# Five block products of seven in each six pairs of the up projections, and one scaling moved behind the down projection

## The chip, the cores and the metric

The kernel runs on one core of one Trainium2 chip, as one program. The metric is the device time of an execution in microseconds (us). Five engines matter: TensorE (PE in the rows, its weight loads PEld), VectorE (DVE), ScalarE (ACT), GpSimd (POOL) and SyncE (SP), which issues the weight transfers.

## The reference

A first block (token mixing and a convolutional feed-forward network) is followed by a second block of two layers, each with a gated feed-forward network. The change touches these two, which the kernel calls `ffn2` and `ffn3`. Everything is float32, with 512 tokens, a model width of 1024 and an inner width of 2816 = 22 x 128:

```python
def rms_norm_2(x, g):
    y = x * lax.rsqrt(jnp.mean(x * x, axis=-1, keepdims=True) + RMS_EPS)
    return y * g

def swiglu_ffn(h, w13, w2):
    g, u = jnp.split(h @ w13, 2, axis=-1)
    return (jax.nn.silu(g) * u) @ w2
# h = h + swiglu_ffn(rms_norm_2(h, ffn_norm_g), w13, w2)
```

## The kernel before, in words

Activations lie transposed: channels on the 128 partitions, 512 tokens along the free dimension (`xT`, eight tiles). Every weight product is made in three passes of a high and a low float32r part (`passes`, lines 382 to 384). So each unit of weights (128 output columns of all 1024 rows, 512 KB) is loaded into one of four buffers `raw`, its high part copied by ACT (`split_hi`, L369) into one of two `whi`, its low part made by DVE (`split_lo`, L377) into one of two `wlo`.

The inverse root of the norm, `rs`, is one number for each token, so it is multiplied in behind the product: DVE evicts a gate or up tile from PSUM as `zS = ps * rs` (L894). ACT applies Silu to the gate half (`act_silu_gate`, L796), DVE multiplies by the up half into `h` (`dve_product`, L899).

An up projection has 22 pairs of a gate and an up unit. Two pairs stand ahead of a loop, two behind it; the loop has `ROUNDS` = 3 iterations of six pairs, ordered by `PATTERN`. False is an ordinary pair: 2 units x 8 slices x 3 passes = 48 matmuls of 512 columns (`pe_pair`). True is a pair by block products (`pe_seven`): the pair is cut in 2 x 2 blocks (halves of the 1024 rows by gate and up columns; the input by halves of the rows and of the tokens), and seven products m1 to m7 of sums of blocks replace eight. A product is 4 slices x 3 passes = 12 matmuls of 256 columns, a pair 84. TensorE takes them in the order m1, m6, m2, m5, m3, m7, m4.

The sums of weight blocks of the next seven pair are prepared one pair ahead, between the additions of the present one. On DVE that is: three sums (`dve_w_sums`, L868 to L871), the low part of two of them (L875, behind ACT's high part L800), the low part of the gate unit (L881), one more difference (L884) and its low part (L888, behind ACT's L804). m1 of the next pair waits for `sums_lo`, which L881 completes. L800 waits for m5 of the present pair, since m5 still reads `w_hi`. So one set of sums can be made ahead and no more.

The seven products are put together by DVE: L912, L913, L916 (behind m2 and m5), L928 (m3), L935 and L937 (m7), L939 (m4), each 256 columns wide. L930 scales the gate half by `rs`, L941 the up half.

In the down projections (`dve_residual`) one of eight output tiles is finished every 22 slices, and DVE adds it to `xT` (L556), which ACT and DVE split again for the next stage (L452, L458).

Of the kernel before, what the change touches and what calls it, by code (L numbers as in the profile page):

```python
# [17 lines left out]
ALU = mybir.AluOpType  # L18
# [6 lines left out]
KT = D // P  # L25
# [94 lines left out]
FIRST = {}  # L120
# [112 lines left out]
    XPART0[_s] = KT * len(XPART0)  # L233
HU, HT = UNIT // 2, T // 2
LAST_PAIRS = 2 * FT - 4
PATTERN = (False, True, True, False, True, True)
ROUNDS = (FT - 4) // len(PATTERN)
SEVENS = ROUNDS * sum(PATTERN)
SEVEN0 = {"ffn2_up": 0, "ffn3_up": 1}
# [6 lines left out]
def build(nc, A, cst_d, out_d, known):  # L246
    ctx = ExitStack()
    with ctx:
# [3 lines left out]
        def sem(name):  # L252
            return ctx.enter_context(nc.semaphore(name))
# [45 lines left out]
        x_read = sem("x_read")  # L299
        sums_made, sums_hi, sums_lo = sem("sums_made"), sem("sums_hi"), sem("sums_lo")  # L300
        block_done, block_kept, block_added = sem("block_done"), sem("block_kept"), sem("block_added")
        S.sems["acc_free"] = acc_free
        x_loaded = [sem(f"x_loaded{i}") for i in range(TT)]
        cst0_loaded, cst_loaded = sem("cst0_loaded"), sem("cst_loaded")
# [239 lines left out]
        def dve_residual(dve, stage, thirds, gain, following=None):  # L544
            per, np_, tiles = round_of(thirds)
            n0 = TILE0[stage]

            def body(i, begun):
                for j in range(per):
                    if begun and j == per - 1:  # L550
                        dve_regain(dve, begun, range(5))
                    if j % np_ == np_ - 1:
                        m = j // np_
                        dve.wait_ge(unit_used, FIRST[stage] + j + 1 + per * i)
                        x = tile_of(xT, m + tiles * i)
                        v.tensor_tensor(x, acc(m), x, ALU.add).then_inc(acc_free, 1)  # L556
                    if begun and j == per - 1:
                        dve_regain(dve, begun, range(5, KT))
                        if not thirds:
                            dve_last_square(dve, stage)  # L560
                    split_lo(dve, FIRST[stage] + j + 2, i, per)
                    if j % np_ == np_ - 1 and gain:
                        dve.wait_ge(acc_free, n0 + m + 3 + tiles * i)
                        dve_gained(dve, gain, m + tiles * i, XPART0[gain] + m + 1 + tiles * i)
            rounds(dve, stage, KT // tiles, body, following)
# [142 lines left out]
                    also()  # L708

        def pe_seven(pe, stage, u, i, s, in_row):  # L710
            n0, a0 = TILE0[stage] + u - 2, nth(stage, i, s, 7) - 7
            u += FIRST[stage]

            def multiply(n, w, x):
                (xh, xl), wh, wl = x_part(x), w_part(whi, w_hi, u, w), w_part(wlo, w_lo, u, w)
                for k in range(4):
                    cols = slice(k * P, (k + 1) * P)
                    last = passes(seven_bank(stage, n), wh[:, cols], wl[:, cols], xh[:, k, :], xl[:, k, :],
                                  k == 0, k == 3)
                return last  # L720
            if in_row:
                pe.wait_ge(block_added, a0 + 2)
            else:
                pe.wait_ge(acc_free, in_units(n0 + 2, i))
            pe.wait_ge(sums_lo, nth(stage, i, s, 2) + 2)
            multiply("m1", "g0", "x11").then_inc(block_done, 1)
            for n in X_SUMS:
                pe.wait_ge(*after(f"{stage} {n} lo"))
            multiply("m6", "s2", "t2")
            multiply("m2", "g1", "x21").then_inc(unit_used, 1)  # L730
            if in_row:
                pe.wait_ge(block_added, a0 + 6)
            multiply("m5", "s1", "t1").then_inc(block_done, 1)
            pe.wait_ge(lo_split, in_units(u + 1, i))
            multiply("m3", "s4", "x22").then_inc(block_done, 1)
            pe.wait_ge(lo_split, in_units(u + 2, i))
            multiply("m7", "s3", "t3").then_inc(block_done, 1)
            if in_row:
                pe.wait_ge(block_added, a0 + 7)
            multiply("m4", "u1", "t4").then_inc(unit_used, 1)  # L740

        def pe_up_seven(pe, stage, name, gain, residual):
# [51 lines left out]
        def act_silu_gate(act, stage, u, i, zS, yg):  # L794
            act.wait_ge(acc_free, in_units(TILE0[stage] + u + 3, i))
            a.activation(yg[:, u // 2 % 2, :], zS[:, 0, :], ACT.Silu).then_inc(gated, 1)  # L796

        def act_two_sums_hi(act, stage, i, s):
            act.wait_ge(sums_made, nth(stage, i, s, 4) + 2)
            a.activation(w_hi[:, 0:2, :], xg[:, :, :], ACT.Copy).then_inc(sums_hi, 1)  # L800
# [5 lines left out]
        def act_pair(act, stage, n, i, zS, yg):  # L806
            special, following = PATTERN[n], PATTERN[(n + 1) % len(PATTERN)]
            u, s, per = 4 + 2 * n, sum(PATTERN[:n]), 2 * len(PATTERN)
            b0 = nth(stage, i, s, 4)
            if special:  # L810
                act.wait_ge(sums_made, b0 + 3)
            split_hi(act, FIRST[stage] + u + 1, i, per)
            if special:
                act.wait_ge(block_done, b0 + 1)
                act.wait_ge(acc_free, in_units(TILE0[stage] + u + 1, i))
                a.activation(kept["m1"], seven_bank(stage, "m1"), ACT.Copy).then_inc(block_kept, 1)
                if following:
                    act.wait_ge(block_done, b0 + 2)
            if following:
                act_two_sums_hi(act, stage, i, s + special)  # L820
            split_hi(act, FIRST[stage] + u + 2, i, per)
            if special and following:
                act.wait_ge(block_done, b0 + 3)
                act_last_sum_hi(act, stage, u + 2, i, s + special)
            act_silu_gate(act, stage, u, i, zS, yg)
            if following and not special:
                act_last_sum_hi(act, stage, u + 2, i, s + special)

        def act_begin_seven(act, stage, name, gain):
            a.preload_act_table_set("natural_log_exp_and_others")  # L830
# [4 lines left out]
        def act_up_seven(act, stage, h, h_hi, zS, yg):  # L835
            u0 = FIRST[stage]
            a.preload_act_table_set("silu_and_others")
            act_silu_gate(act, stage, 0, None, zS, yg)
            act_x_sums_hi(act, stage, ("t1",))
            split_hi(act, u0 + 3)  # L840
            act_x_sums_hi(act, stage, ("t3", "t2"))
            split_hi(act, u0 + 4)
            act_silu_gate(act, stage, 2, None, zS, yg)
            act_x_sums_hi(act, stage, ("t4",))
            with act.Fori(0, ROUNDS) as i:
                for n in range(len(PATTERN)):
                    act_pair(act, stage, n, i, zS, yg)
            u = LAST_PAIRS
            split_hi(act, u0 + u + 1)
            for j, tiles in enumerate((range(0, 6), range(6, 12), range(12, 17), range(17, 21))):  # L850
                for m in tiles:
                    act_product_hi(act, stage, m, h, h_hi)
                split_hi(act, u0 + u + j + 2)
                if j % 2 == 0:
                    act_silu_gate(act, stage, u + j, None, zS, yg)
            act_product_hi(act, stage, FT - 1, h, h_hi)
# [32 lines left out]
                            ALU.subtract).then_inc(lo_split, 1)  # L889

        def dve_up_unit(dve, stage, u, i, j, odd, zS):
            dve.wait_ge(unit_used, in_units(FIRST[stage] + u + j + 1, i))
            dve.wait_ge(prod_done, in_pairs(PAIR0[stage] + u // 2 + 2, i))
            v.tensor_tensor(zS[:, j, :], pair_bank(stage, odd, j), rs[:, :], ALU.mult).then_inc(acc_free, 1)  # L894

        def dve_product(dve, stage, u, i, h, zS, yg):
            dve.wait_ge(acc_free, in_units(TILE0[stage] + u + 4, i))
# [4 lines left out]
        def dve_pair(dve, stage, n, i, h, zS, yg):  # L902
            special, following = PATTERN[n], PATTERN[(n + 1) % len(PATTERN)]
            u, s, per = 4 + 2 * n, sum(PATTERN[:n]), 2 * len(PATTERN)
            u0, b0, a0 = FIRST[stage] + u, nth(stage, i, s, 4), nth(stage, i, s, 7)
            split_lo(dve, u0 + 1, i, per)
            if following:
                dve_w_sums(dve, stage, u + 2, i, s + special)
# [24 lines left out]
            if special:  # L933
                dve.wait_ge(block_done, b0 + 4)
                v.tensor_tensor(kept["u3"], seven_bank(stage, "m7"), kept["u2"], ALU.add).then_inc(block_added, 1)  # L935
                dve.wait_ge(block_added, a0 + 5)
                v.tensor_tensor(zS[:, 1, HT:T], seven_bank(stage, "m5"), kept["u3"], ALU.add).then_inc(block_added, 1)  # L937
                dve.wait_ge(unit_used, in_units(u0 + 2, i))
                v.tensor_tensor(zS[:, 1, 0:HT], seven_bank(stage, "m4"), kept["u3"], ALU.add).then_inc(block_added, 1)  # L939
                dve.wait_ge(block_added, a0 + 7)  # L940
                v.tensor_tensor(zS[:, 1, :], zS[:, 1, :], rs[:, :], ALU.mult).then_inc(acc_free, 1)  # L941
            else:
                dve_up_unit(dve, stage, u, i, 1, 0, zS)
            dve_product(dve, stage, u, i, h, zS, yg)
# [2090 lines left out]
```

## Time and profile before

| | |
|---|---|
| time, three runs | 1831.75 us median (1831.74 to 1834.98) |
| profiled execution | 1835.28 us, its span 1833.5 us |
| TensorE's granted clock | 0.999 |
| busy PE, DVE, ACT | 98%, 62%, 42% |
| DMA | 161.19 MB, 88 GB/s |
| up projection `ffn2`, loop | 945.3 to 1131.6 us, three rounds of 62.1 us |

A row of the timeline gives start and duration from the span's start. The time between two starts can be shorter than the duration, since instructions of one engine overlap at their ends. Ends of matmuls are modelled, so for TensorE the distance between starts is to be read.

### The profile page before, as it was taken

How to read it: one execution, taken by the hardware profiler on the slowest of the kernel's cores; microseconds unless marked ns; L12 is line 12 of the kernel's file. 1: busy time of each engine (PE TensorE's matmuls, PEld its weight loads, DVE VectorE, ACT ScalarE, POOL GpSimd, SP SyncE). 2: the span in 40 equal slices, each digit the busy share in tenths (PEclk: the TensorE clock that was granted, in tenths of full speed). 3: DMA queues.
4: the chain of work that ended last, by engine and by line, in shares of the span. 5: the costliest groups of instructions: out<-in, count | busy, mean ns of one | idle time of the engine just before them, and what ended most of it. 6: DMA issues, size and time to landing. Idle time of an engine off the chain costs nothing.

```text
span 1833.5 us, 29524 instructions
## 1 busy us (share of the span) xinstructions
PE 1801.9 (98%) x10927; PEld 1499.9 (82%) x10927; DVE 1128.0 (62%) x1670; ACT 775.4 (42%) x1155; POOL 146.9 (8%) x134
## 2 busy tenths in 40 slices
PE   7999999999999999999999999999999999999998
PEld 6787676688888888888889999888776789999887
DVE  6553677467676633445588888533757398888422
ACT  6635436454444422322354335323555363345322
POOL 0030001111111100000200000001000200000010
PEclk9999999999999999999999999999999999999999
DMA  6311212133333333333333333333230233333331
GB/s 196 81 38 48 59 36 81 35 92 95 100 92 102 87 97 102 94 103 93 98 98 102 96 102 100 95 95 105 77 91 1 69 92 104 103 102 96 94 101 66
DMA packets 309240, 161.19 MB, mean 88 GB/s; under 512 B 12688, under 2 KB 306832, under 8 KB 309024
## 3 DMA queue, kind: packets, MB, share of 16 engines
q1 hardware_dynamic: 308080, 157.28, 30.0%
q0 software_dynamic: 640, 2.17, 0.4%
q8 instruction: 61, 1.00, 0.2%
q10 hardware_dynamic: 432, 0.52, 0.1%
q14 instruction: 27, 0.22, 0.0%
HBM read 157.85 MB, written 2.10 MB: 87 GB/s over the span
## 4 chain that ended last, share of the span: by engine, by line
PE 96%; DVE 2%; ACT 1%; issue 1%; DMA 0%; ACTq 0%; DVEq 0%
PE ps L382 28%; PE ps L384 28%; PE ps L383 28%; PE ps L2125 1%; PE ps L1536 1%; PE ps L2442 1%; PE ps L2443 1%; PE ps L2116 1%; PE ps L1447 1%; PE ps L1853 1%; PE ps L1269 1%; PE ps L1797 1%; PE ps L1841 0%; PE ps L2222 0%; PE ps L2223 0%
## 5 line engine op out<-in xcount | busy, mean ns | idle before, releaser
L382 PE MATMUL ps<-xhi,whi 128*128 128x512 f32 (+1 forms) x1464 | 558.7, 382 | 2.0 <-DVE xlo L1176 1.1
L384 PE MATMUL ps<-xhi,wlo 128*128 128x512 f32 (+1 forms) x1464 | 550.2, 376 | 0.0
L383 PE MATMUL ps<-xlo,whi 128*128 128x512 f32 (+1 forms) x1464 | 550.0, 376 | 0.0
L369 ACT ACTIVATE whi<-raw 128x1024 fp32r<-128x1024 f32 (+2 forms) x297 | 308.4, 1039 | 528.2 <-PE ps L384 527.8
L377 DVE TENSOR_TENSOR wlo<-raw,whi 128x1024 fp32r<-128x1024 f32 (+2 forms) x273 | 335.3, 1228 | 231.2 <-ACT whi L369 231.2
L382 PEld LDWEIGHTS ps<-xhi,whi 128*128 128x128 f32 x1464 | 275.8, 188 | 55.9 <-issue 4.6
L383 PEld LDWEIGHTS ps<-xlo,whi 128*128 128x128 f32 x1464 | 275.9, 188 | 50.9 <-issue 3.1
L384 PEld LDWEIGHTS ps<-xhi,wlo 128*128 128x128 f32 x1464 | 275.7, 188 | 50.3
L576 POOL TENSOR_TENSOR ssq<-ssq,sq 128x512 f32<-128x512 f32 x45 | 72.1, 1602 | 990.5 <-ACT sq L523 990.5
L384 PE MATMUL ps<-h_lo,wlo 128*128 128x512 f32 x352 | 136.9, 389 | 0.0
L382 PE MATMUL ps<-h_lo,whi 128*128 128x512 f32 x352 | 136.9, 389 | 0.0
L383 PE MATMUL ps<-h_hi,whi 128*128 128x512 f32 x352 | 136.9, 389 | 0.0
L556 DVE TENSOR_TENSOR xT<-ps,xT 128x512 f32<-128x512 f32 (+1 forms) x48 | 33.2, 691 | 120.1 <-PE ps L384 120.1
L382 PEld LDWEIGHTS ps<-h_lo,whi 128*128 128x128 f32 x352 | 66.1, 188 | 13.9
L384 PEld LDWEIGHTS ps<-h_lo,wlo 128*128 128x128 f32 x352 | 66.1, 188 | 13.7
L383 PEld LDWEIGHTS ps<-h_hi,whi 128*128 128x128 f32 x352 | 66.1, 188 | 13.6
L382 PE MATMUL ps<-h_hi,whi 128*128 128x512 f32 x176 | 68.5, 389 | 0.0
L383 PE MATMUL ps<-h_lo,whi 128*128 128x512 f32 x176 | 68.5, 389 | 0.0
L384 PE MATMUL ps<-h_hi,wlo 128*128 128x512 f32 x176 | 68.5, 389 | 0.0
L800 ACT ACTIVATE w_hi<-xg 128x1024 fp32r<-128x1024 f32 x24 | 25.5, 1063 | 89.3 <-PE ps L384 48.3
L648 DVE TENSOR_TENSOR zS<-ps,rs 128x512 f32<-128x512 f32 x44 | 30.4, 692 | 43.8 <-PE ps L384 41.4
L458 DVE SCALAR_TENSOR_TENSOR xlo<-xT,pcol,xhi 128x512 fp32r<-128x512 f32 (+1 forms) x48 | 47.0, 1009 | 12.6 <-ACT xhi L452 12.6
(389 smaller groups left out, 2760.6 us busy)
## 6 DMA issues: line engine op xcount, KB each, us to landing
raw<-in_conv_ffn_w SPq DMA_DIRECT2D x52, 512.0 KB, 3.8
raw<-in_mla_ffn_w SPq DMA_DIRECT2D x52, 512.0 KB, 3.8
raw<-in_w_up SPq DMA_DIRECT2D x44, 512.0 KB, 3.8
raw<-in_w_in SPq DMA_DIRECT2D x28, 512.0 KB, 3.8
raw<-in_conv_w_in SPq DMA_DIRECT2D x24, 512.0 KB, 3.8
raw<-in_w_down SPq DMA_DIRECT2D x16, 448.0 KB, 3.7
raw<-in_conv_ffn_w SPq DMA_DIRECT2D x16, 448.0 KB, 3.7
raw<-in_mla_ffn_w SPq DMA_DIRECT2D x16, 448.0 KB, 3.7
```

Of the source, the lines that this page charges most:

```text
L369: a.activation(whi[:, u % PARTS, 0:n], raw[:, u % RAW, 0:n], ACT.Copy).then_inc(hi_split, 1)
L377: e.tensor_tensor(wlo[:, u % PARTS, 0:n], raw[:, u % RAW, 0:n], f32(whi[:, u % PARTS, 0:n]), ALU.subtract).then_inc(lo_split, 1)
L382: t_.matmul(out, wh, xh, start=first, stop=False)
L383: t_.matmul(out, wh, xl, start=False, stop=False)
L384: return t_.matmul(out, wl, xh, start=False, stop=last)
L458: v.scalar_tensor_tensor(tile_of(xlo, k), tile_of(xT, k), gain_of(name, k), f32(tile_of(xhi, k)), ALU.mult, ALU.subtract).then_inc(x_lo, 1)
L556: v.tensor_tensor(x, acc(m), x, ALU.add).then_inc(acc_free, 1)
L576: g.tensor_tensor(ssq[:, :], ssq[:, :], sq[:, m, :], ALU.add).then_inc(summed, 1)
L648: v.tensor_tensor(z, acc(j), rs[:, :], ALU.mult).then_inc(acc_free, 1)
L800: a.activation(w_hi[:, 0:2, :], xg[:, :, :], ACT.Copy).then_inc(sums_hi, 1)
L1269: t_.matmul(out, C("hsum"), sq[:, i % 2, :], start=True, stop=True).then_inc(*step("pe", f"{name} sum{i} full"))
L1447: last = t_.matmul(chunk(out, n)[rows], chunk(lhs, c)[rows], chunk(rhs, c)[rows], start=True, stop=True)
```

## The change

`PATTERN` has five pairs of seven products in six. The up half is no longer scaled in either kind of pair: in an ordinary pair ACT copies it out of PSUM (`act_up_half`), in a pair of seven L941 goes. Since `rs` belongs to the token, it can be multiplied in behind the down projection: `dve_residual` scales each output tile (L561 of the new kernel) and then adds it to `xT` (L563). PSUM banks of m4 are now guarded by `acc_free`.

```diff
-PATTERN = (False, True, True, False, True, True)
+PATTERN = (False, True, True, True, True, True)
...
+            scaled = {"ffn2_down": 0, "ffn3_down": KT}.get(stage)
...
-                        v.tensor_tensor(x, acc(m), x, ALU.add).then_inc(acc_free, 1)
+                        if scaled is None:
+                            v.tensor_tensor(x, acc(m), x, ALU.add).then_inc(acc_free, 1)
+                        else:
+                            v.tensor_tensor(xg[:, m % 2, :], acc(m), rs[:, :], ALU.mult).then_inc(out_scaled, 1)
+                            dve.wait_ge(out_scaled, scaled + m + 1 + tiles * i)
+                            v.tensor_tensor(x, xg[:, m % 2, :], x, ALU.add).then_inc(acc_free, 1)
...
             if in_row:
-                pe.wait_ge(block_added, a0 + 7)
+                pe.wait_ge(acc_free, in_units(n0 + 4, i))
             multiply("m4", "u1", "t4").then_inc(unit_used, 1)
...
+        def act_up_half(act, stage, u, i, odd, zS):
+            act.wait_ge(unit_used, in_units(FIRST[stage] + u + 2, i))
+            act.wait_ge(prod_done, in_pairs(PAIR0[stage] + u // 2 + 2, i))
+            a.activation(zS[:, 1, :], pair_bank(stage, odd, 1), ACT.Copy).then_inc(acc_free, 1)
...
             if following and not special:
                 act_last_sum_hi(act, stage, u + 2, i, s + special)
+            if not special:
+                act_up_half(act, stage, u, i, 0, zS)
...
                 for m in tiles:
                     act_product_hi(act, stage, m, h, h_hi)
+                if j % 2:
+                    act_up_half(act, stage, u + j - 1, None, j // 2, zS)
...
         def dve_up_unit(dve, stage, u, i, j, odd, zS):
-            dve.wait_ge(unit_used, in_units(FIRST[stage] + u + j + 1, i))
-            dve.wait_ge(prod_done, in_pairs(PAIR0[stage] + u // 2 + 2, i))
-            v.tensor_tensor(zS[:, j, :], pair_bank(stage, odd, j), rs[:, :], ALU.mult).then_inc(acc_free, 1)
+            if j == 0:
+                dve.wait_ge(unit_used, in_units(FIRST[stage] + u + 1, i))
+                dve.wait_ge(prod_done, in_pairs(PAIR0[stage] + u // 2 + 2, i))
+                v.tensor_tensor(zS[:, 0, :], pair_bank(stage, odd, 0), rs[:, :], ALU.mult).then_inc(acc_free, 1)
...
-                v.tensor_tensor(zS[:, 1, 0:HT], seven_bank(stage, "m4"), kept["u3"], ALU.add).then_inc(block_added, 1)
-                dve.wait_ge(block_added, a0 + 7)
-                v.tensor_tensor(zS[:, 1, :], zS[:, 1, :], rs[:, :], ALU.mult).then_inc(acc_free, 1)
+                v.tensor_tensor(zS[:, 1, 0:HT], seven_bank(stage, "m4"), kept["u3"], ALU.add).then_inc(acc_free, 1)
+                dve.wait_ge(block_added, a0 + 6)
```

DVE at the end of a pair of seven, as the program of before has it (`ISA` and `REGISTER_ALU` are steps of the sequencer alone):

```order
L939 TENSOR_TENSOR zS<-ps,sq 128x256 [waits unit_used]
L940 REGISTER_ALU
L941 TENSOR_TENSOR zS<-zS,rs 128x512 [waits block_added]
L897 REGISTER_ALU
L898 REGISTER_ALU [waits acc_free]
L899 ISA [waits gated]
L899 TENSOR_TENSOR h<-yg,zS 128x512
```

And the same place in the changed kernel, whose line numbers are 19 higher here:

```order
L958 TENSOR_TENSOR zS<-ps,sq 128x256 [waits unit_used]
L959 REGISTER_ALU
L916 REGISTER_ALU [waits block_added]
L917 REGISTER_ALU [waits acc_free]
L918 ISA [waits gated]
L918 TENSOR_TENSOR h<-yg,zS 128x512
```

The scaling is gone and the product stands directly behind the last addition, with its waits.

ACT at the end of an ordinary pair in the loop, from the Silu to the high part of the next pair's up unit, before:

```order
L796 ACTIVATE yg<-zS 128x512 [waits acc_free]
L803 REGISTER_ALU
L804 ACTIVATE w_hi<-raw 128x512 [waits sums_made]
L811 REGISTER_ALU
L366 REGISTER_ALU [waits sums_made]
L368 REGISTER_ALU [waits unit_loaded0]
L369 ACTIVATE whi<-raw 128x1024 [waits unit_used]
```

And in the changed kernel:

```order
L803 ACTIVATE yg<-zS 128x512 [waits acc_free]
L815 REGISTER_ALU
L816 ACTIVATE w_hi<-raw 128x512 [waits sums_made]
L806 REGISTER_ALU
L807 ISA [waits unit_used]
L808 ACTIVATE zS<-ps 128x512 [waits prod_done]
L823 REGISTER_ALU
L367 REGISTER_ALU [waits sums_made]
L370 ACTIVATE whi<-raw 128x1024 [waits unit_used,unit_loaded0]
```

The copy out of PSUM (L808) stands between them and waits for the pair's last matmul; the high part of the next up unit is queued behind it.

## Rows read from the trace of the kernel before

**Rows 1.** The page: the chain that ended last, by engine
```profile
PE 96%; DVE 2%; ACT 1%; issue 1%; DMA 0%; ACTq 0%; DVEq 0%
```

**Rows 2.** Windows: stretch, its us, busy (x instructions) by engine, clock, DMA
```profile
956.18:966.25 10.07, 10.07 (x85) 10.07 (x84) 8.40 (x12) 3.46 (x4) 0.00 (x0) 1.00 0.36 104
976.33:987.24 10.91, 10.91 (x50) 9.02 (x49) 9.13 (x12) 4.35 (x5) 0.00 (x0) 1.00 0.29 85
945.30:1007.40 62.10, 62.10 (x434) 58.34 (x433) 53.38 (x81) 24.10 (x30) 0.00 (x0) 1.00 0.34 98
```

**Rows 3.** Timeline, DVE: start us, us, line, operation, shape, idle before
```profile
957.33 0.69 DVE L899 TENSOR_TENSOR h<-yg,zS 128x512 f32 x1 [0.26 <-DVE zS L894]
957.94 1.22 DVE L377 TENSOR_TENSOR wlo<-raw,whi 128x1024 fp32r<-128x1024 f32 x1
959.07 0.69 DVE L868 TENSOR_TENSOR xg<-raw 128x512 f32<-128x512 f32 x1
959.79 0.69 DVE L870 TENSOR_TENSOR xg<-xg,raw 128x512 f32<-128x512 f32 x1
960.40 0.69 DVE L871 TENSOR_TENSOR raw<-raw 128x512 f32<-128x512 f32 x1
961.00 0.42 DVE L912 TENSOR_TENSOR sq<-ps,sq 128x256 f32<-128x256 f32 x1
961.34 0.42 DVE L913 TENSOR_TENSOR zS<-ps,sq 128x256 f32<-128x256 f32 x1
962.24 0.42 DVE L916 TENSOR_TENSOR sq<-ps,sq 128x256 f32<-128x256 f32 x1 [0.48 <-PE ps L384]
963.32 1.23 DVE L875 TENSOR_TENSOR w_lo<-xg,w_hi 128x1024 fp32r<-128x1024 f32 x1 [0.66 <-ACT w_hi L800]
964.47 1.22 DVE L881 TENSOR_TENSOR wlo<-raw,whi 128x1024 fp32r<-128x1024 f32 x1
965.72 0.69 DVE L884 TENSOR_TENSOR raw<-raw,xg 128x512 f32<-128x512 f32 x1
966.33 0.42 DVE L928 TENSOR_TENSOR zS<-ps,sq 128x256 f32<-128x256 f32 x1
966.78 0.69 DVE L930 TENSOR_TENSOR zS<-zS,rs 128x512 f32<-128x512 f32 x1
967.39 0.68 DVE L888 TENSOR_TENSOR w_lo<-raw,w_hi 128x512 fp32r<-128x512 f32 x1
967.99 0.42 DVE L935 TENSOR_TENSOR sq<-ps,sq 128x256 f32<-128x256 f32 x1
968.44 0.42 DVE L937 TENSOR_TENSOR zS<-ps,sq 128x256 f32<-128x256 f32 x1
968.78 0.41 DVE L939 TENSOR_TENSOR zS<-ps,sq 128x256 f32<-128x256 f32 x1
969.23 0.69 DVE L941 TENSOR_TENSOR zS<-zS,rs 128x512 f32<-128x512 f32 x1
970.18 0.69 DVE L899 TENSOR_TENSOR h<-yg,zS 128x512 f32 x1 [0.25 <-DVE zS L941]
970.79 1.22 DVE L377 TENSOR_TENSOR wlo<-raw,whi 128x1024 fp32r<-128x1024 f32 x1
```

**Rows 4.** Timeline, ACT, same stretch
```profile
956.38 1.06 ACT L369 ACTIVATE whi<-raw 128x1024 fp32r<-128x1024 f32 x1 [1.52 <-PE ps L384]
962.23 1.06 ACT L800 ACTIVATE w_hi<-xg 128x1024 fp32r<-128x1024 f32 x1 [4.03 <-PE ps L384]
966.45 0.64 ACT L804 ACTIVATE w_hi<-raw 128x512 fp32r<-128x512 f32 x1 [2.20 <-DVE raw L884]
```

**Rows 5.** The page, costliest groups: one weight load
```profile
L382 PEld LDWEIGHTS ps<-xhi,whi 128*128 128x128 f32 x1464 | 275.8, 188 | 55.9 <-issue 4.6
```

**Rows 6.** Timeline, end of the second network's first down projection
```profile
1273.42 0.69 DVE L556 TENSOR_TENSOR xT<-ps,xT 128x512 f32 x1 [2.56 <-PE ps L384]
...
1275.99 1.32 DVE L458 SCALAR_TENSOR_TENSOR xlo<-xT,pcol,xhi  x1 [0.38 <-ACT xhi L452]
...
1277.86 0.39 PE L382 MATMUL ps<-xhi,whi 128*128 128x512 f32 x1
```

**Rows 7.** Chain of waits in order of time, the kernel's end
```profile
1821.54 0.70 DVE xT L556
```

More of the change, by code:

```diff
@@ L301, in build @@
         block_done, block_kept, block_added = sem("block_done"), sem("block_kept"), sem("block_added")
+        out_scaled = sem("out_scaled")
         S.sems["acc_free"] = acc_free
@@ L710, in pe_seven @@
         def pe_seven(pe, stage, u, i, s, in_row):
-            n0, a0 = TILE0[stage] + u - 2, nth(stage, i, s, 7) - 7
+            n0, a0 = TILE0[stage] + u - 2, nth(stage, i, s, 6) - 6
             u += FIRST[stage]
@@ L839, in act_up_seven @@
             act_x_sums_hi(act, stage, ("t1",))
+            act_up_half(act, stage, 0, None, 0, zS)
             split_hi(act, u0 + 3)
@@ L844, in act_up_seven @@
             act_x_sums_hi(act, stage, ("t4",))
+            act_up_half(act, stage, 2, None, 1, zS)
             with act.Fori(0, ROUNDS) as i:
@@ L904, in dve_pair @@
             u, s, per = 4 + 2 * n, sum(PATTERN[:n]), 2 * len(PATTERN)
-            u0, b0, a0 = FIRST[stage] + u, nth(stage, i, s, 4), nth(stage, i, s, 7)
+            u0, b0, a0 = FIRST[stage] + u, nth(stage, i, s, 4), nth(stage, i, s, 6)
             split_lo(dve, u0 + 1, i, per)
```

## The prediction

> **What bounds the kernel now.** I read the chain of waits first: TensorE holds 96% of it, DVE 2% [rows 1]. A change pays only where TensorE gets less to do or is made to wait. Next I read the windows over the loop of the `ffn2` up projection. A pair by seven products takes TensorE 10.07 us, an ordinary pair 10.91 us, and a round of four and two 62.10 us, with no gap: 4 x 10.07 + 2 x 10.91 = 62.1 [rows 2]. In that round DVE is busy 53.4 us and ACT 24.1 us [rows 2]. By these averages nothing but TensorE matters. The timeline of DVE through one pair of seven that also prepares the next says something else [rows 3]. From its first instruction (L377 at 957.94) to that of the next pair (970.79) it takes 12.85 us, longer than TensorE's 10.07. That goes well today because such a pair is never followed by another: the next pair of seven prepares nothing, and the ordinary pair leaves DVE time. The change puts four such pairs in a row. So the forecast rests on one number, how long DVE needs for such a pair when it is the one that is late.
>
> **TensorE's gain.** One ordinary pair in each round becomes one of seven: 10.91 - 10.07 = 0.84 us [rows 2]. There are three rounds in each of two networks, so 6 x 0.84 = 5.0 us, if nothing waits.
>
> **DVE's period in a row of preparing pairs.** Count start to start [rows 3]. In the 12.85 us stand two waits that are TensorE's and ACT's doing and not DVE's: L916 starts 0.90 behind L913, waiting for m5, and L875 starts 1.08 behind L916, waiting for ACT's L800, which itself waited for m5 [rows 4]. Without a wait a 256-column addition is followed after 0.34 (L912 to L913). That takes off 0.56 + 0.74 = 1.30 and leaves 11.55. The change takes L941 away. From L939 to the product it is now 1.40 (968.78 to 970.18): 0.45 to L941, its 0.69, and a gap of 0.25-0.26 before the product, which waits for the result in front of it. Without L941 the product waits for L939 instead: 0.42 + 0.25 = 0.67. Saved 0.73, so the period is 11.55 - 0.73 = 10.82 us. That is still 0.75 more than TensorE's 10.07.
>
> Would the two waits stay, or others take their place? Take L875 of one pair as zero. L881 ends at 1.15 + 1.22 = 2.37 and releases m1 of the next pair; its m5, the fourth product, is done 6.05 later (962.23 - 956.18, from the start of the pair to ACT's L800 [rows 2, 4]), at 8.4. DVE's L870 of that pair comes at 7.47 (963.32 to 970.79) - 0.73 + 1.85 = 8.59 and ends at 9.28; ACT's 1.06 brings 10.4, and L875 is due at 10.82. So L800 is hidden, by 0.4 us. L804 comes 1.40 behind L884's start (0.69, 0.03, 0.64 and 0.03 [rows 3, 4]) and L888 is due at 1.67: hidden by 0.27. m7 and m4 of that pair are over by 12.9, and its L939 is due at 10.82 + 5.46 = 16.3. No other wait is late next.
>
> **Where TensorE waits.** Let a round's first pair of seven start at zero. Its L875 starts at 963.32 - 956.18 = 7.14 [rows 2, 3] and is still set by TensorE's m5. The second pair's follows at 17.96, the third's at 28.78, the fourth's at 39.60. The fourth's L881 ends 2.37 later, at 41.97; for the way to TensorE I add 0.1, between 0.03 (ACT's L800 ends at 963.29, L875 starts at 963.32 [rows 3, 4]) and 0.22, that plus a weight load of 0.19 no longer hidden [rows 5]. The fifth pair starts at 42.07 instead of 4 x 10.07 = 40.3. TensorE loses 1.75 to 1.8 us: about 0.25 before the third pair and 0.75 before the fourth and the fifth each. Before the second it loses nothing (L881 ends at 9.5, TensorE is free at 10.07). The fifth prepares nothing, and the ordinary pair gives DVE time to be early again. A round becomes 62.10 - 0.84 + 1.75 = 63.0 us, +0.91; six rounds +5.5 us.
>
> The Trainium skill, page "VectorE: DVE Perf Modes", section "The DRAIN you can't avoid", says that semaphores between chained Vector instructions cost nothing extra. By it, L941 is worth only the spacing of two such instructions. This trace disagrees: L930 comes 0.45 behind L928, for whose result it waits, where an addition without such a wait comes after 0.34, and the product comes 0.95 behind L941 [rows 3]. By the rule the sum would be that of the upper bound below, +8.6 us.
>
> **Bounds of the saving.** The trace does not show the product directly behind a 256-column addition. At least L941's plain spacing goes, 0.61 (L884 to L928): period 10.94, loss 2.11, a round +1.27, together +8.6 with the ends below. At most the product comes 0.45 behind L939 as L941 did, saved 0.95: period 10.60, loss 1.09, +2.5 us in all. I take 0.73, since the product stands 0.25 or 0.26 behind the end of what it waits for in both of its rows, behind an eviction and behind L941 [rows 3]. With the way to TensorE at 0.03 or 0.22 the ends are +2.1 and +9.3.
>
> **The up half on ACT.** In an ordinary pair ACT copies 512 columns, some 0.65 us like L804 [rows 4], instead of DVE's 0.69; the product waits for either and starts at about the same time, 957.3. Queued behind the copy is L369, which started at 956.38 [rows 4] and now starts near 957.0, ending at 958.0; L377 follows at 958.1 instead of 957.94. L916 waits 0.48 for m5 anyway [rows 3], which hides the 0.15. Without that cover it would be 0.15 x 6 = 0.9 us. In the pairs ahead of and behind the loop the copy delays a `split_hi` by 0.65, with several microseconds until TensorE wants it. I set all of this at zero. The copy's further wait, for the last product, was over a pair earlier. The new guard of m4 waits for L939 of the pair before, which is when the old one opened.
>
> **The down projections.** Sixteen tiles get one more DVE instruction of 0.69, with the addition behind it waiting for it; behind that stand the low parts of the weights. A tile is 22 x 3 = 66 matmuls of 10.91 / 48 = 0.227 us [rows 2], so one comes every 15 us, and fourteen of them are free. At the kernel's end the addition is on the chain [rows 7]: +0.69 + 0.03 = 0.7 us. At the end of `ffn2` the last tile's low part starts at 1275.99 and ends at 1277.31, and TensorE wants it at 1277.86 [rows 6]. The addition comes 0.94 later in a loop (0.69 and the gap of 0.25), so the part ends near 1278.1: +0.3 us. It could be 0 or 0.9. Ends together +1.0.
>
> **The sum.** +5.5 + 1.0 = +6.5 us: the profiled execution of 1835.28 us would become 1841.8. It stands 3.5 above the median of the runs, and the steps are the same in both, so I lay the sum on the median: 1831.75 + 6.5 = 1838.2 us.
>
> **Rivals.** The averages decide (0.12). DVE's work in a round goes from 53.4 to about 51.7 us: the seven pair's 11.5 against the ordinary one's 9.1 [rows 2, 3], less six scalings of 0.69. That is far under TensorE's 61.3. If the preparation can be early enough, the gain of 5.0 stays less the ends of 1.0: 1827.7 us, faster. For it: DVE idles 8.7 us a round today [rows 2]. Against it: those idle times lie in other pairs, and L800 cannot start before m5. Its point is a period of 10.24 us; below that no pair waits.
>
> A smaller period that just eats the gain (0.12): at 10.46 us the loss is 0.67 a round and the total is nothing, 1832 us. It would take 0.36 less than I count, if starts close up when DVE never idles. Nothing in the rows closes up so far: every 512-column instruction without a wait takes 0.60 to 0.61 [rows 3].
>
> The handshakes with ACT and TensorE stay (0.04). If the 1.30 us of waits stand in each pair even when DVE is late, the period is 12.12, the loss 5.65 a round, +28.9 + 1.0: 1861.6 us. The margins of 0.4 and 0.27 speak against it.
>
> **How the numbers follow.** My forecast has 0.72. Its own range is 1833.9 to 1841.1 us. The range given is 1831 to 1842: it takes in the case of no change and leaves out the averages (0.12) and the handshakes (0.04). A measurement tells 0.2%, 3.7 us, from no change. Faster holds the averages and a little, 0.13. Same, to 1835.4, holds the smaller period and the low end of my own range, 0.16. Slower is 0.71.
>
> **What would show it.** In the profile after, the windows of a round show 63.0 us (61.3 if the averages are right). TensorE's first matmul of the third, fourth and fifth pair of seven has idle time before it, ended by DVE's `wlo` of the gate unit, of some 0.25, 0.75 and 0.75 us. The `w_lo` instruction of two halves starts 10.8 us apart from pair to pair and waits for ACT only in the first. The product starts 0.67 behind the last addition. The last `xT` comes 0.7 later behind the last matmul. I am wrong if the period is under 10.5, or if TensorE waits at m3, m7 or m5 rather than at m1.

## The result, and the profile after

The changed kernel takes 1843.22 us (median of five runs, 1840.95 to 1845.16), the kernel before 1833.38 us beside it (five runs, 1831.74 to 1834.98). The ratio is 1.0051, with a 95% interval of 1.0035 to 1.0068: slower by 9.4 us, between 6.4 and 12.5. Forecast were +6.5 us and 1838.2 us, with a range to 1842. So the sign and the mechanism came out, and the size was 3 us short. The median of before, from three runs 1831.75 us, moved up by 1.6 us with two more.

First the page after: the chain by engine, which answers [rows 1], and TensorE's largest group with its idle time and what ended it.

```profile
PE 85%; DVE 9%; issue 3%; ACT 2%; DVEq 0%; DMA 0%; ACTq 0%
L383 PE MATMUL ps<-xhi,whi 128*128 128x512 f32 (+1 forms) x1416 | 536.5, 379 | 8.0 <-DVE wlo L899 5.7
```

DVE's share went from 2% to 9%. The 7% more are about 129 us, far more than was lost: where TensorE waits for DVE in the end, the chain runs back through DVE's whole queue.

The window of one round of `ffn2`, from the first DVE `w_lo` of the round to the same of the next, answers the third row of [rows 2]: stretch, its us, then busy (x instructions) of PE, PEld, DVE, ACT, POOL, clock, DMA share, GB/s.

```profile
960.29:1023.28 62.99, 62.07 (x470) 59.57 (x470) 56.24 (x89) 25.93 (x35) 0.00 (x0) 1.00 0.35 101
```

A round takes 62.99 us; forecast was 63.0, and the averages would have had 61.3. DVE does more in a round than before: 89 instructions and 56.2 us busy against 81 and 53.4 [rows 2]. The new pair of seven prepares the next one, as the ordinary pair did, but now the pair in front of it prepares too. The prediction had DVE's work fall to 51.7; it counted the new pair and left out the one in front. (Busy time also holds the instructions' overlapping ends, in both kernels.)

DVE's timeline through a preparing pair that follows another answers [rows 3]: start us, us, line, operation, shape, idle time before. L893 is the old L875, L899 the old L881, L918 the product.

```profile
960.29 1.23 DVE L893 TENSOR_TENSOR w_lo<-xg,w_hi 128x1024 fp32r<-128x1024 f32 x1 [0.66 <-ACT w_hi L812]
961.44 1.22 DVE L899 TENSOR_TENSOR wlo<-raw,whi 128x1024 fp32r<-128x1024 f32 x1
...
965.75 0.41 DVE L958 TENSOR_TENSOR zS<-ps,sq 128x256 f32<-128x256 f32 x1
966.42 0.69 DVE L918 TENSOR_TENSOR h<-yg,zS 128x512 f32 x1 [0.26 <-DVE zS L958]
967.03 1.22 DVE L378 TENSOR_TENSOR wlo<-raw,whi 128x1024 fp32r<-128x1024 f32 x1
968.17 0.68 DVE L886 TENSOR_TENSOR xg<-raw 128x512 f32<-128x512 f32 x1
968.89 0.69 DVE L888 TENSOR_TENSOR xg<-xg,raw 128x512 f32<-128x512 f32 x1
969.50 0.68 DVE L889 TENSOR_TENSOR raw<-raw 128x512 f32<-128x512 f32 x1
970.10 0.42 DVE L931 TENSOR_TENSOR sq<-ps,sq 128x256 f32<-128x256 f32 x1
970.43 0.41 DVE L932 TENSOR_TENSOR zS<-ps,sq 128x256 f32<-128x256 f32 x1
970.76 0.41 DVE L935 TENSOR_TENSOR sq<-ps,sq 128x256 f32<-128x256 f32 x1
971.10 1.21 DVE L893 TENSOR_TENSOR w_lo<-xg,w_hi 128x1024 fp32r<-128x1024 f32 x1
...
981.88 1.22 DVE L893 TENSOR_TENSOR w_lo<-xg,w_hi 128x1024 fp32r<-128x1024 f32 x1
...
992.66 1.22 DVE L893 TENSOR_TENSOR w_lo<-xg,w_hi 128x1024 fp32r<-128x1024 f32 x1
```

Both waits of [rows 3] are there in the first pair and gone in the next: L935 comes 0.33 behind L932, and L893 0.34 behind L935. The period is 10.81, 10.78 and 10.78 us. The product starts 0.67 behind the last addition.

What TensorE does meanwhile, by its weight loads (which are real records, while ends of matmuls are modelled), at the first matmul of the third, fourth and fifth pair of seven:

```profile
973.50 0.19 PEld L383 LDWEIGHTS ps<-xhi,whi 128*128 128x128 f32 x1 [0.24 <-DVE wlo L899]
...
984.28 0.19 PEld L383 LDWEIGHTS ps<-xhi,whi 128*128 128x128 f32 x1 [0.65 <-DVE wlo L899]
...
995.06 0.19 PEld L383 LDWEIGHTS ps<-xhi,whi 128*128 128x128 f32 x1 [0.65 <-DVE wlo L899]
```

From one of these to the next are 10.78 us, where TensorE alone needs 10.07 [rows 2]. So it loses 0.71 us and not only the 0.65 of idle time, and in the round 62.99 - 61.26 = 1.73 us (61.26 is a round without waits, 62.10 - 0.84).

The two ends that the prediction priced: the last tile of `ffn2`'s down projection, which answers [rows 6], and the chain's row at the kernel's end, which answers [rows 7], now two instructions.

```profile
1274.11 0.69 DVE L563 TENSOR_TENSOR xT<-xg,xT 128x512 f32 x1
...
1276.67 0.97 DVE L459 SCALAR_TENSOR_TENSOR xlo<-xT,pcol,xhi  x1 [0.74 <-ACT xhi L453]
...
1277.83 0.39 PE L383 MATMUL ps<-xhi,whi 128*128 128x512 f32 x1
...
1824.99 0.69 DVE L561 TENSOR_TENSOR xg<-ps,rs 128x512 f32<-128x512 f32 x1 [7.39 <-PE ps L385]
1825.72 0.69 DVE L563 TENSOR_TENSOR xT<-xg,xT 128x512 f32<-128x512 f32 x1
```

### Where the time is, section by section

Each of the five norms has its sum, one pair of matmuls (L410, now L411) that all kernels have. In the two profiled executions these sums divide the span:

| section | before | after | difference |
|---|---|---|---|
| to the first sum (code that the change leaves alone) | 393.13 | 390.11 | -3.02 |
| from there to the sum behind `ffn2` | 885.42 | 888.40 | +2.98 |
| between the two networks' sections | 197.70 | 197.74 | +0.04 |
| `ffn3`, to DVE's first instruction of the last tile | 345.29 | 348.74 | +3.45 |
| from there to the end of the span | 11.96 | 14.1 | +2.1 |

The second row is called `ffn2`'s section below. Its first 535.0 us, to the sum ahead of `ffn2` (928.10 before, 925.07 after), are other stages, the same in all ten profiles of this study to 0.04 us; its differences are those of `ffn2`.

The first row isn't the change's: the same instructions took 389.4 to 393.1 us in the ten profiles, and the profiled execution of before had a granted clock of 0.91 between 260 and 280 us, where the one of after had 1.00. Without it the spans are apart by 1839.1 - 1833.5 + 3.0 = 8.6 us. That fits the timed 9.4, and it splits into four terms:

- The loops, 2.61 + 3.04 = 5.65 us (to the last eviction of the up projections).
- The starts of the down projections, 0.42 each, 0.84 us.
- DVE's extra instruction at the end, 0.73 us (1824.99 to 1825.72).
- TensorE's last transposes, about 1.3 us in these two executions.

The second was not foreseen at all. Three engines' timelines of after at that place, ACT, DVE and the weight loads:

```profile
1153.20 0.60 ACT L808 ACTIVATE zS<-ps 128x512 f32<-128x512 f32 x1 [1.71 <-PE ps L385]
1153.69 0.95 ACT L370 ACTIVATE whi<-raw 128x896 fp32r<-128x896 f32 x1
...
1162.31 1.09 DVE L378 TENSOR_TENSOR wlo<-raw,whi 128x896 fp32r<-128x896 f32 x1
...
1163.44 0.19 PEld L383 LDWEIGHTS ps<-h_lo,whi 128*128 128x128 f32 x1 [0.51 <-DVE wlo L378]
```

And the two of before that correspond to the second and third of these rows, ACT and DVE:

```profile
1153.68 0.96 ACT L369 ACTIVATE whi<-raw 128x896 fp32r<-128x896 f32 x1 [1.77 <-PE ps L384]
...
1162.30 1.09 DVE L377 TENSOR_TENSOR wlo<-raw,whi 128x896 fp32r<-128x896 f32 x1
```

The weight load that wants it in before, with the one in front:

```profile
1163.17 0.19 PEld L384 LDWEIGHTS ps<-h_lo,wlo 128*128 128x128 f32 x1
1163.44 0.19 PEld L382 LDWEIGHTS ps<-h_lo,whi 128*128 128x128 f32 x1
```

The start times of the two kernels look alike by chance: TensorE begins this down projection at 1153.42 in before and at 1153.00 in after, so in after DVE's rows are 0.42 later against TensorE's. Before, ACT's split of a weight unit starts when TensorE has released the buffer. Now the copy of the last up half (L808) starts then, and the split 0.49 later. Behind that split stand on DVE its low part, the last product and ten low parts of `h`, and only then the low part of the down projection's third unit. In before that part was just in time: the weight load that wants it starts at 1163.44 too, 0.27 behind the load in front of it, where 0.23 is the rhythm. In after 0.69 lie between the two (1162.75 to 1163.44), so 0.42 more.

The windows of the last microseconds, after (1826 to 1839) and before (1822 to 1828):

```profile
1826.00:1832.00 6.00, 3.73 (x27) 3.41 (x26) 2.94 (x5) 4.95 (x8) 0.00 (x0) 0.77 0.13 47
1832.00:1839.00 7.00, 1.24 (x6) 0.84 (x4) 1.08 (x2) 0.69 (x1) 0.00 (x0) 0.50 0.70 262
```

```profile
1822.00:1828.00 6.00, 4.22 (x36) 3.67 (x34) 3.26 (x6) 5.59 (x9) 0.00 (x0) 1.00 0.15 57
```

In after the granted clock was 0.77 over the first of these stretches and 0.50, its lower level of 1.2 GHz, in the second; in before it stayed at 1.00 over the transposes. TensorE's rows for the last twelve, of after and of before:

```profile
1830.42 2.82 PE L2654 MATMUL ps<-cst,xT 128*128 128x128 f32 x12 [1.42 <-ACT fin L2668]
```

```profile
1826.25 1.53 PE L2636 MATMUL ps<-cst,xT 128*128 128x128 f32 x12 [1.42 <-ACT fin L2650]
```

### The profile page after: what moved, and what is told of

Same layout as the page of the kernel before. It is cut to its first block, busy times and chain, and to the rows that moved or that the text cites. A ratio compares the mean times of both kernels' runs of the same rounds, so it can differ in the third digit from the quotient of the medians.

```text
span 1839.1 us, 30175 instructions
## 1 busy us (share of the span) xinstructions
PE 1801.4 (98%) x11143; PEld 1507.3 (82%) x11143; DVE 1145.5 (62%) x1720; ACT 790.6 (43%) x1187; POOL 143.4 (8%) x134
## 4 chain that ended last, share of the span: by engine, by line
PE 85%; DVE 9%; issue 3%; ACT 2%; DVEq 0%; DMA 0%; ACTq 0%
PE ps L383 25%; PE ps L384 25%; PE ps L385 25%; PE ps L2143 1%; DVE wlo L899 1%; DVE wlo L378 1%; PE ps L1554 1%; PE ps L2460 1%; PE ps L2461 1%; PE ps L2134 1%; DVE raw L889 1%; PE ps L1465 1%; PE ps L1871 1%; DVE h_hi L966 1%; PE ps L1287 1%
## 5 line engine op out<-in xcount | busy, mean ns | idle before, releaser
L383 PE MATMUL ps<-xhi,whi 128*128 128x512 f32 (+1 forms) x1416 | 536.5, 379 | 8.0 <-DVE wlo L899 5.7
L385 PE MATMUL ps<-xhi,wlo 128*128 128x512 f32 (+1 forms) x1416 | 526.0, 371 | 0.0
L384 PE MATMUL ps<-xlo,whi 128*128 128x512 f32 (+1 forms) x1416 | 525.9, 371 | 0.0
L378 DVE TENSOR_TENSOR wlo<-raw,whi 128x1024 fp32r<-128x1024 f32 (+2 forms) x267 | 328.0, 1228 | 229.2 <-ACT whi L370 228.9
L383 PEld LDWEIGHTS ps<-xhi,whi 128*128 128x128 f32 x1416 | 266.6, 188 | 62.1 <-DVE wlo L899 9.7
L384 PEld LDWEIGHTS ps<-xlo,whi 128*128 128x128 f32 x1416 | 266.8, 188 | 46.9 <-issue 3.1
L385 PEld LDWEIGHTS ps<-xhi,wlo 128*128 128x128 f32 x1416 | 266.7, 188 | 46.5
L559 DVE TENSOR_TENSOR xT<-ps,xT 128x512 f32<-128x512 f32 (+1 forms) x32 | 22.1, 691 | 75.7 <-PE ps L385 75.7
L383 PE MATMUL ps<-t_hi,w_hi 128*128 128x256 f32 x240 | 67.9, 283 | 0.0
L384 PE MATMUL ps<-t_lo,w_hi 128*128 128x256 f32 x240 | 67.9, 283 | 0.0
```

The costliest lines, as they stand in the source:

```text
L378: e.tensor_tensor(wlo[:, u % PARTS, 0:n], raw[:, u % RAW, 0:n], f32(whi[:, u % PARTS, 0:n]), ALU.subtract).then_inc(lo_split, 1)
L383: t_.matmul(out, wh, xh, start=first, stop=False)
L384: t_.matmul(out, wh, xl, start=False, stop=False)
L385: return t_.matmul(out, wl, xh, start=False, stop=last)
```

## The experiments

The theory: in a row of preparing pairs DVE needs 10.8 us for a pair where TensorE needs 10.07, and TensorE pays the difference at m1. The rivals are that the pattern is not the cause (the scaling behind the down projections, or ACT's copy), that averages decide, and that another engine could take DVE's load at no cost. All ratios are against the kernel before, run beside on the same chip.

### Everything but the pattern

```diff
-PATTERN = (False, True, True, True, True, True)
+PATTERN = (False, True, True, False, True, True)
```

> The changed kernel with the old order of pairs (four of seven in six, never two preparing ones in a row). Theory (DVE's period in a row of preparing pairs costs the time): rounds of 62.1 us again; what stays is the rest of the change, of which the traces show 0.7 us for the second instruction at the kernel's end, 0.4 us at the start of each down projection (TensorE waits for the low part of the third unit, queued on DVE behind ten low parts of products) and perhaps 1.4 us for transposes at the granted clock 0.5 at the very end: +1.5 to +2.9 us against the kernel before. Rival (the moved scaling and ACT's copies are what costs): the time stays near that of the changed kernel, +9 us.

Measured: 1834.76 us against 1832.22, ratio 1.0010 (1.0001 to 1.0019), +1.8 us. The profile has +0.38 in `ffn2`'s section, +0.31 in `ffn3`'s and the 0.73 at the end. So the pattern carries most of the loss. The moved scaling and ACT's copy cost 1.4 us by the profile and 1.8 by the timing, whose interval runs from 0.2 to 3.5; the prediction had 1.0. The wait at the start of the down projections is there without the pattern: the page of this run has "<-DVE wlo L378 1.0" at their weight loads, as after has and before hasn't. It is the copy's or the scaling's, then. The rows above say the copy's, and in after the first scaling of an output tile (L561) starts only at 1168.55, 5 us behind that wait.

### The pattern alone

The kernel before, with the new `PATTERN`; the up half is still scaled by DVE.

> The kernel before with five pairs of seven in six and nothing else: DVE still scales the up half. Theory: the period of a preparing pair is 11.55 us when DVE is late, TensorE loses 7.14 + 3 x 11.55 + 2.47 - 40.30 = 3.96 us in a round and gains 0.84, six rounds: +18.7 us. Rival (the averages over a round decide, DVE is busy 56 of 61 us): -5.0 us.

Measured: 1855.27 us against 1832.22, ratio 1.0125 (1.0109 to 1.0140), +22.9 us. DVE's timeline, its `w_lo` instruction from pair to pair:

```profile
961.83 1.23 DVE L875 TENSOR_TENSOR w_lo<-xg,w_hi 128x1024 fp32r<-128x1024 f32 x1 [0.66 <-ACT w_hi L800]
...
973.35 1.21 DVE L875 TENSOR_TENSOR w_lo<-xg,w_hi 128x1024 fp32r<-128x1024 f32 x1
...
985.21 1.21 DVE L875 TENSOR_TENSOR w_lo<-xg,w_hi 128x1024 fp32r<-128x1024 f32 x1
...
996.72 1.21 DVE L875 TENSOR_TENSOR w_lo<-xg,w_hi 128x1024 fp32r<-128x1024 f32 x1
```

The period is 11.52, 11.86 and 11.51 us; the prediction's working gives 11.55. (In the 11.86 the product starts 0.35 later than in the others, for no reason that the trace names.) Against 10.79 with L941 gone, a 512-column instruction and its waits for results cost 0.73 us in the pair, as forecast. In the profile `ffn2`'s section is 9.71 us longer than before's and `ffn3`'s 9.05, together 18.8, which is the expectation's 18.7. The timed difference is 4 us more. In the profile 1.7 of them lie behind the last tile, 1.1 of these in the last transposes; the rest isn't found. Against the averages this run says less than its expectation has it: DVE is busy 60.1 us in a round here (the window from 961.83 to 1027.03), not 56, which is nearly TensorE's 61.3. The next run is the test of them.

### Three in a row

The kernel before, with four of six pairs as it had, in another order.

```diff
-PATTERN = (False, True, True, False, True, True)
+PATTERN = (False, True, True, True, False, True)
```

> The kernel before with its four pairs of seven of six put as three in a row and one alone, so that every count of instructions is that of before. Theory: the third pair of a row starts 7.14 + 11.55 + 2.47 - 20.15 = 1.0 us late in each round, +6.0 us in six rounds. Rival (averages): no change.

Measured: 1839.07 us against 1832.22, ratio 1.0035 (1.0022 to 1.0049), +6.4 us. This is the sharpest test of the averages: TensorE's and DVE's work in a round is what it was (DVE busy 53.8 us in both, in windows from `w_lo` to `w_lo`), and only their order differs. `ffn2`'s section is 3.02 us longer and `ffn3`'s 2.94, together 6.0 as expected. The page, TensorE's weight loads:

```profile
L382 PEld LDWEIGHTS ps<-xhi,whi 128*128 128x128 f32 x1464 | 275.5, 188 | 61.4 <-DVE wlo L881 5.7 <-issue 4.1 <-ACT mx L1399 0.8
```

TensorE loses 5.7 us to `wlo` in six rounds, one wait in each (0.96 at 975.05 in this round), where the same row of before has none [rows 5]. The averages are refuted.

### The product on GpSimd

The kernel after, with the loops' product h = silu(gate) x up taken from DVE. DVE saves about 0.9 us in each pair, and the period would come to 9.9, under TensorE's 10.07. DVE also gets a wait for the product ahead of its additions, which is not in the cut below.

```diff
+        def pool_pair_products(pool, stage, h, zS, yg):
+            with pool.Fori(0, ROUNDS) as i:
+                for n in range(len(PATTERN)):
...
+                    g.tensor_tensor(tile_of(h, in_pairs(u // 2, i)), yg[:, u // 2 % 2, :], zS[:, 1, :],
+                                    ALU.mult).then_inc(prod_done, 1)
```

> The changed kernel with the product of the gate and up half (128x512) moved from DVE to GpSimd inside the loops. Theory: DVE's period falls from 10.80 by 0.67 + 0.61 - 0.34 = 0.94 to 9.86 us, under TensorE's 10.07; rounds of 61.3 us, no wait of TensorE for the low part of the gate unit, -5.0 us and the ends of +1.5 to +2.9: 2 to 3.5 us under the kernel before. Rival (GpSimd and DVE slow each other on SBUF): DVE's instructions beside the product are longer than 0.69 and 1.22 us and the period stays above 10.07; above 10.5 nothing is gained against the kernel before.

Measured: 1843.81 us against 1832.22, ratio 1.0063 (1.0049 to 1.0077), +11.5 us, no better than after: the expectation's rival came true. The timelines of DVE and GpSimd:

```profile
965.40 1.23 DVE L378 TENSOR_TENSOR wlo<-raw,whi 128x1024 fp32r<-128x1024 f32 x1
965.74 2.03 POOL L935 TENSOR_TENSOR h<-yg,zS 128x512 f32 x1 [10.83 <-DVE zS L976]
966.54 1.78 DVE L890 TENSOR_TENSOR xg<-raw 128x512 f32<-128x512 f32 x1
```

L890 takes 1.78 us beside the product and 0.68 in the kernel after (L886 there). The product takes 2.03 where it takes 1.30 in the next experiment. The rows read as turns: GpSimd waits for L378 to end near 966.5, works until 967.77, and L890 makes its 0.6 us behind it. The period is 10.96 us. In this window DVE never idles for the added wait. The Trainium skill, page "SBUF — State Buffer", section "SBUF: two separate sides", says that GpSimd and a DVE instruction with two SBUF inputs take one pair of ports as an exclusive lock for a whole instruction. The trace agrees: the product takes 0.73 us longer and L890 1.10.

### The same, timed

The product waits until DVE has made its three weight sums, so that it falls beside the additions that read PSUM. For this DVE's own wait for the product had to go behind most of its additions, ahead of the first write into the up half of `zS`, with a wait for the Silu in its old place. The cut shows only GpSimd's new wait.

```diff
+                    if n + 2 < len(PATTERN):
+                        pool.wait_ge(sums_made, nth(stage, i, sum(PATTERN[:n + 2]), 4) + 3)
```

> The product on GpSimd as in the run before, but in the row of preparing pairs it waits for the third sum of weights of the next pair, so that it runs beside DVE's three additions out of PSUM (1.0 us) and not beside instructions with two SBUF operands. Theory (GpSimd and DVE exclude each other on SBUF pairs, the price was 1.1 us in one instruction): at most 0.45 us are left to stretch the next w_lo, the period falls from 10.95 to 9.9 to 10.3 us, TensorE waits at most 0.1 us in a round, rounds of 61.3 to 61.5 us: 2 to 3.5 us under the kernel before, 11 to 14 under the run before. Rival (DVE is stretched whatever it reads): the period stays at 10.9 and the time at that of the run before, +11 us against the kernel before.

Measured: 1834.46 us against 1833.74, ratio 1.0006 (0.9996 to 1.0015), +1.1 us: 2 to 3.5 us of gain were expected, and none came. DVE and GpSimd again:

```profile
972.16 0.42 DVE L951 TENSOR_TENSOR sq<-ps,sq 128x256 f32<-128x256 f32 x1
972.44 1.30 POOL L937 TENSOR_TENSOR h<-yg,zS 128x512 f32 x1 [9.77 <-DVE raw L893]
972.50 0.41 DVE L952 TENSOR_TENSOR zS<-ps,sq 128x256 f32<-128x256 f32 x1
972.83 0.41 DVE L955 TENSOR_TENSOR sq<-ps,sq 128x256 f32<-128x256 f32 x1
973.38 1.45 DVE L897 TENSOR_TENSOR w_lo<-xg,w_hi 128x1024 fp32r<-128x1024 f32 x1
...
983.46 1.66 DVE L897 TENSOR_TENSOR w_lo<-xg,w_hi 128x1024 fp32r<-128x1024 f32 x1
```

The additions keep their 0.41 to 0.42 us; L897, with two inputs in SBUF, is drawn out from 1.22 by what is left of the product. The periods are 10.08, 10.08 and 10.30 us, and a round, by the windows from 963.30 to 1024.81, takes 61.51 us. With DVE's period at TensorE's own, the loops gain what the prediction's averages promised, less 0.25: `ffn2`'s section is 1.4 us below before, `ffn3`'s 1.0. The periods and the round came as expected, then, and the ends take the gain back. In the profile the part from DVE's first instruction of the last tile to the span's end is 14.3 us, against 12.0 in before. DVE's extra instruction is 0.73 of that, the transposes are alike (1.53 us), and 1.6 come behind DVE's last instruction, where only the output's transfer is left: 6.6 us against 4.9. That last piece runs from 3.6 to 6.6 us in the ten profiles, and no row says why.

### The tail

The low parts of the last four `h` tiles of each up projection on GpSimd, so that DVE's low part of the third down unit is early again. Once on top of the timed product, once on the kernel after alone.

```diff
-            for m in range(16, FT):
+            for m in range(16, 18):
...
+        def pool_last_lows(pool, stage, h, h_hi, h_lo):
+            pool.wait_ge(prod_lo, PAIR0[stage] + 18 + 2)
+            for m in range(18, FT):
+                pool.wait_ge(prod_hi, PAIR0[stage] + m + 1)
+                g.tensor_tensor(h_lo[:, m, :], h[:, m, :], f32(h_hi[:, m, :]), ALU.subtract).then_inc(prod_lo, 1)
```

> The same, and the last four low parts of products (18 to 21) on GpSimd, so that DVE is free 2.4 us earlier for the low part of the down projection's third unit. Theory: TensorE's wait of 0.42 us at the start of each down projection goes, 0.8 us under the same kernel without this: 3 to 4.5 us under the kernel before. Rival (that wait is nothing, the 0.4 us come from elsewhere): no difference.

> The changed kernel with only the last four low parts moved to GpSimd. Theory: 0.8 us under the changed kernel (which is 9.4 over the kernel before by its ratio): +8.5 us, and in its trace the first output tile of each down projection 0.4 us nearer to the last gate tile. Rival: no difference, +9.4 us.

Measured with the product: 1832.90 us against 1833.74, ratio 0.9996 (0.9987 to 1.0005), where 3 to 4.5 us of gain were expected. Alone: 1841.29, ratio 1.0040 (1.0028 to 1.0053), +7.3 us where +8.5 was. The intervals, some 2 us to either side, are too wide to show 0.8 us. The profiles do: in them the two sections lose 0.37 and 0.43 us against the kernel without it, and on the kernel after 0.39 and 0.51, of 0.42 expected for each. The weight loads of the down projections in the kernel with the tail alone have no wait for DVE left, where after has "<-DVE wlo L378 1.0":

```profile
L383 PEld LDWEIGHTS ps<-h_lo,whi 128*128 128x128 f32 x352 | 66.1, 188 | 13.8
```

That settles the unforeseen term. The version with both is the best one found. By the two ratios it is 10 us faster than the change as made, and it can't be told from the kernel before.

### Without the scaling of the gate half

The kernel after without L949 in pairs of seven. This leaves a part of the computation out; it asks what becomes late next when DVE needs 0.7 us less. ACT's Silu gets a wait of its own for the addition in front, not in the cut.

```diff
-                dve.wait_ge(block_added, a0 + 4)
-                v.tensor_tensor(zS[:, 0, :], zS[:, 0, :], rs[:, :], ALU.mult).then_inc(acc_free, 1)
```

> The changed kernel with one DVE instruction less in each pair of seven: the gate half is not scaled either there (part of the computation is left out). Theory (only DVE's period counts): the period falls by 0.45 + 0.61 - 0.34 = 0.72 to 10.07 us, just TensorE's own 10.07, the three waits of a round go, rounds of 61.3 us; -5.0 us, the ends +1.5 to +2.9: 2 to 3.5 us under the kernel before, 11 to 13 under the changed one. Rival (a row of preparing pairs makes TensorE wait for ACT or for PSUM banks, whatever DVE does): rounds stay above 62.5 us and the time within 3 us of the changed kernel.

Measured: 1837.21 us against 1833.74, ratio 1.0022 (1.0013 to 1.0031), +4.0 us; 2 to 3.5 us under the kernel before were expected. DVE's timeline in the second pair:

```profile
972.37 1.22 DVE L895 TENSOR_TENSOR w_lo<-xg,w_hi 128x1024 fp32r<-128x1024 f32 x1
973.50 1.22 DVE L901 TENSOR_TENSOR wlo<-raw,whi 128x1024 fp32r<-128x1024 f32 x1
974.75 0.69 DVE L904 TENSOR_TENSOR raw<-raw,xg 128x512 f32<-128x512 f32 x1
...
976.14 0.69 DVE L908 TENSOR_TENSOR w_lo<-raw,w_hi 128x512 fp32r<-128x512 f32 x1 [0.36 <-ACT w_hi L816]
...
982.87 1.21 DVE L895 TENSOR_TENSOR w_lo<-xg,w_hi 128x1024 fp32r<-128x1024 f32 x1
```

The period falls from 10.78 to 10.50 us, not to the 10.07 of TensorE. L908 (after's L906) now waits 0.36 us for ACT's high part, which comes 1.39 behind L904 whatever DVE does. This is the handshake for which the prediction counted a margin of 0.27: take 0.7 away from in front of it and 0.4 comes back as a wait. So the expectation failed by its size, by not asking what is late next.

## Why the prediction was right or wrong

- **What bounds.** Right. The kernel before was TensorE's, and the change made four preparing pairs DVE's. Three in a row shows it with the same work.
- **The period.** 10.82 us forecast, 10.78 to 10.81 measured, with both old waits gone from the second pair on. The 0.73 for L941 is confirmed by the two kernels with and without it (11.52 and 10.79). By the Trainium skill's rule that the semaphore costs nothing ("VectorE: DVE Perf Modes", "The DRAIN you can't avoid") it would have been 10.94; the trace disagrees.
- **Where TensorE waits.** Right. 0.25, 0.75 and 0.75 forecast, 0.24, 0.65 and 0.65 measured by the idle time of the weight loads. By the distance of their starts it is 0.71 for each of the last two, which leaves 0.31 for the first, 1.73 in all against 1.75. A round of 63.0 was 62.99. The way from DVE to TensorE, set at 0.1, was 0.05 (L899 ends at 973.45, the load starts at 973.50).
- **The loops' sum.** 5.5 forecast, 5.65 in the profiles. `ffn3`'s three rounds had slightly more than `ffn2`'s; the profiles differ by that much from one another.
- **The averages, the smaller period, the handshakes.** All three fell. For the averages the working had DVE's busy time wrong, 51.7 us in a round where 56.2 was measured; even so it is under TensorE's 61.3, so the rival stays what it was, and three in a row is what decides against it. The handshakes are real but were hidden by the counted margins; the last experiment shows that they were thin.
- **The copy on ACT.** This step failed: a term set at zero that has a price. It said that behind the loop the copy delays a `split_hi` by 0.65, "with several microseconds until TensorE wants it", and set it at zero. The weights of that split had the time. DVE's queue behind it had not, and its last member was wanted at once (ready at 1162.31 + 1.09 = 1163.40, loaded at 1163.44). Measured: 0.42 us for each network, 0.84 in all; moving four low parts off DVE takes it away in the trace.
- **The end of `ffn2`.** Forecast +0.3, measured nothing. L459 started 0.68 later than L458 and took 0.97 instead of 1.32, so it ended 0.33 later, at 1277.64, just in front of the weight load that wants it at 1277.69 (and 1277.64 in before). Both durations look drawn out by GpSimd's sum of squares beside them: it ended at 1276.76 in before and at 1277.09 in after, in each L458 or L459 ended 0.55 behind it, and the shortest of their kind took 0.74. That fits the turn-taking of the GpSimd experiment, which the working left out; no run tests it here.
- **The kernel's end.** 0.7 forecast, 0.73 measured. The 1.3 us of slower transposes came on top, a term that the working doesn't have. It isn't shown that the change causes them. The twelve last transposes took 1.53 us in before and 2.82 in after; in the experiments, in the order above, 1.64, 2.63, 2.51, 2.82, 1.53, 1.81, 2.82 and 2.33. Kernels with the extra instruction in front of them stand on both sides, and so do those with before's end. What sets the clock there stays open.
- **The base and the range.** The range's upper end of 1842 was made from bounds of the loops' terms, and left 0.9 us above the largest of them for all the places whose cost was set at zero. The time came out 1.2 above it. The sum was laid on a three-run median that stood 1.6 us under that of five. On the latter it would have been 1839.9; of the missing 3.3, 0.84 are the copy, about 1.3 may be the transposes (seen in one execution of each kernel), and the rest is within what the medians are uncertain by. The copy alone doesn't carry the time out of the range: without it 1842.4 is left. The low base matters as much: laid on the five-run median, the same range would have ended at 1843.6, above the measured time.

## What to carry to other kernels

When an engine with 86% of the bottleneck's load (53.4 of 62.1 us here) must repeat its longest stage several times in a row, work out its period start to start with its waits removed, and compare that with the bottleneck's; the average over the round doesn't show it. Where a step is moved to an engine with room, follow not only the instruction that it delays, but the whole queue of the next engine behind that instruction, to the last item that the bottleneck takes. And when load is taken off, ask at once which handshake has the thinnest margin: of 0.7 us removed in front of a margin of 0.27, about 0.3 were gained.

## What the runs showed of the hardware that I had not expected

GpSimd's 512-column product (1.30 us) left DVE additions that read one input from PSUM as they were (0.41 to 0.42 us each). It drew out a DVE instruction with two inputs in SBUF by 1.10 us when it started beside such instructions, and by 0.2 to 0.4 us where only its end reached one. Waits that set its start took the kernel from a ratio of 1.0063 to 1.0006, some 10 us. The other was the granted clock at the kernel's end, from 1.00 to 0.50 within the same few transposes of kernels that differ elsewhere, worth up to 1.3 us; what decides it stays open.
